# Two-layer encoder with top-2 experts in fp32: slot selections from spread slot numbers, slot weights as row sums, whole weight loads, and two sets of dummy matmuls in the S5 mixer

## What is computed

```python
def _hier_moe(h, w_group, b_group, w_expert, b_expert, w_gate, w_up, w_down):
    ...
    combine = (jax.nn.one_hot(g_idx[:, 0], N_GROUPS, dtype=jnp.float32)[:, :, None]
               * g_val[:, :, None] * within[:, None, :]).astype(h.dtype)
    y = jnp.zeros_like(t)
    for g in range(N_GROUPS):
        a = jnp.einsum('td,edf->tef', t, w_gate[g])
        u = jnp.einsum('td,edf->tef', t, w_up[g])
        act = jax.nn.silu(a) * u * combine[:, g, :, None]
        y = y + jnp.einsum('tef,efd->td', act, w_down[g])
```

## Time and profile before

| | |
|---|---|
| median of 3 runs | 852.99 us (852.57 to 853.74) |
| profiled execution | 855.27 us, its span 853.50 us |
| mean granted TensorE clock | 0.971 |
| TensorE busy | 784.3 us (92%), 4303 matmul records |
| VectorE (DVE) / ScalarE (ACT) / GpSimd (POOL) busy | 379.1 / 282.5 / 143.8 us |
| moved by DMA | 245.54 MB, mean 288 GB/s |

### The profile page before, as it was taken

One profiled execution on the slowest core, in us unless ns is written; L12 is line 12 of the kernel. 1 busy time (PEld: TensorE's weight loads), 2 busy tenths in 40 slices (PEclk: granted clock), 3 DMA queues, 4 the chain that ended last, 5 costly groups with the idle time before them and its releaser, 6 DMA issues.

```text
span 853.5 us, 11150 instructions
## 1 busy us (share of the span) xinstructions
PE 784.3 (92%) x4303; PEld 425.0 (50%) x4303; DVE 379.1 (44%) x701; ACT 282.5 (33%) x522; POOL 143.8 (17%) x135
## 2 busy tenths in 40 slices
PE   3867979999999999989999878998999999999997
PEld 3645845534343343436888644555434434344355
DVE  6998633631222212217868669526222221231164
ACT  5250153521212212216755444433322221221163
POOL 5695510110000000000066554000000000000000
PEclk9896989999999999999999979999999999999999
DMA  6052096799999999997579490266799999999931
GB/s 223 1 156 99 4 327 279 284 337 415 412 413 414 411 415 411 412 405 261 197 166 328 124 269 1 79 266 246 260 403 414 412 414 413 412 415 412 410 138 49
DMA packets 73926, 245.54 MB, mean 288 GB/s; under 512 B 16050, under 2 KB 17136, under 8 KB 65296
## 3 DMA queue, kind: packets, MB, share of 16 engines
q1 hardware_dynamic: 71776, 240.35, 73.2%
q0 software_dynamic: 2096, 4.45, 2.9%
HBM read 243.17 MB, written 1.60 MB: 287 GB/s over the span
## 4 chain that ended last, share of the span: by engine, by line
PE 75%; DVE 8%; DMA 6%; SPq 4%; POOL 4%; ACT 2%; issue 2%; DVEq 0%; ACTq 0%
PE PS L1887 22%; PE PS L1915 12%; PE PS L1662 11%; PE PS L1929 5%; DMA ring<-in_p 5%; PE PS L1821 3%; PE PS L2163 3%; PE PS L1776 2%; PE PS L2138 2%; PE PS L2117 2%; PE PS L1836 2%; PE PS L2049 2%; SPq L466 1%; PE PS L1755 1%; POOL qrs L693 1%
## 5 line engine op out<-in xcount | busy, mean ns | idle before, releaser
L1887 PE MATMUL PS<-ring,xw 128*64 128x512 f32 x1024 | 226.2, 593 | 2.9 <-DVE act L1395 1.5
L1887 PEld LDWEIGHTS PS<-ring,xw 128*64 128x64 f32 x1024 | 73.6, 137 | 146.5 <-issue 143.3
L1915 PE MATMUL PS<-ring,actT 128*64 128x512 f32 x512 | 122.4, 603 | 1.3 <-DVE actT L1389 0.7
L588 POOL TENSOR_TENSOR rstd<-ms,mhalf 128x2 f32<-128x2 f32 x6 | 4.3, 710 | 570.7 <-DVE ms L1053 564.5
L902 ACT ACTIVATE ohi<-PS 128x512 fp32r<-128x512 f32 x64 | 38.2, 597 | 160.4 <-PE PS L1915 160.4
L1389 DVE COPY actT<-PS 128x256 f32<-128x256 f32 x32 | 13.6, 424 | 166.7 <-PE PS L1898 159.1
L1078 DVE SCALAR_TENSOR_TENSOR ringr<-ring,gcol,dwh 128x512 fp32r<-128x512 f32 x80 | 62.7, 834 | 26.9 <-ACT dwh L753 25.8
L1403 DVE TENSOR_TENSOR olo<-PS,ohi 128x512 fp32r<-128x512 f32 x64 | 44.1, 689 | 67.1 <-ACT ohi L902 65.7
L894 ACT ACTIVATE act<-PS,wslot 128x256 f32<-128x256 f32 x32 | 15.2, 474 | 158.9 <-PE PS L1887 158.9
L753 ACT ACTIVATE dwh<-ring,gcol 128x512 fp32r<-128x512 f32 x80 | 52.8, 716 | 35.0 <-PE PS L1662 34.2
L1662 PE MATMUL PS<-ringr,hTh 128*128 128x512 f32 x160 | 63.2, 395 | 0.0
(11 more groups left out here) (332 smaller groups left out, 1067.2 us busy)
## 6 DMA issues: line engine op xcount, KB each, us to landing
ring<-in_moe_w_gate SPq DMA_DIRECT2D x128, 512.0 KB, 15.9
ring<-in_moe_w_up SPq DMA_DIRECT2D x128, 512.0 KB, 16.4
ring<-in_moe_w_down SPq DMA_DIRECT2D x64, 1024.0 KB, 17.0
ring<-in_nat_w_qkv SPq DMA_DIRECT2D x6, 2048.0 KB
ring<-in_ple_w_gate SPq DMA_DIRECT2D x4, 2048.0 KB
ring<-in_s_w_out SPq DMA_DIRECT2D x2, 2048.0 KB
ring<-in_nat_w_o SPq DMA_DIRECT2D x2, 2048.0 KB
ring<-in_s_w_in SPq DMA_DIRECT2D x1, 2048.0 KB
```

What stands on the lines that cost most here:

```text
L1887: ins = mm(PS[CAP * h_:CAP * h_ + CAP, 0, :].rearrange("p (u f) -> p u f", u=2), xw[:, p % 2, k, CAP * h_:CAP * h_ + CAP], wv[h_][:, k], s ...
L1915: ins = mm(PS[CAP * h_:CAP * h_ + CAP, 2 + n, :], actT[:, k, CAP * h_:CAP * h_ + CAP], wd[h_][:, k, 512 * n:512 * n + 512], start=k == 0, ...
```

## The change

Selections: TensorE spreads the slot numbers of all tokens over the partitions once a layer (`slot_rows`: a matmul of the slot column, repeated 128 times, with the identity), DVE keeps them in `slotrow`. For a pair DVE compares them with the number of the slot that a partition stands for (`pid`) and so has the transposed selection without a transpose. Slot weights: token weights and norms are spread in the same way (`weight_rows`), and a slot's weight is the sum of a row, accumulated while selection and row are multiplied. `MIX` and its semaphores go. SP: gate and up are loaded whole, except for pairs 3 and 4. The transposes of p move behind down(15). POOL: an iota and a copy for `pid`, and the router of layer 1 loaded behind the norm of PLE 0, since `rstdrow` now lies where the router does. S5: two sets of `keep_busy(4)`.

```diff
             def load_early(n):
 
                 s, (gate_, up_, _) = items[n]
-                if prev[n] is not None:
-                    name, value = done[prev[n]]
-                    sp.wait_ge(S("gu_half" if name == "gu_done" else name), value)
                 sp.dma_start(ring[s][:, 0:1024], gate_[1][:, 0:1024]).then_inc(loaded[s], 32)
                 sp.dma_start(ring[s][:, 2048:3072], up_[1][:, 0:1024]).then_inc(loaded[s], 16)
...
+            def load_gate_up(n):
                 s, (gate_, up_, _) = items[n]
                 if prev[n] is not None:
                     name, value = done[prev[n]]
                     sp.wait_ge(S(name), value)
+                sp.dma_start(ring[s][:, 0:2048], gate_[1]).then_inc(loaded[s], 32)
+                sp.dma_start(ring[s][:, 2048:4096], up_[1]).then_inc(loaded[s], 16)
...
-                    if p < NP:
+                    if p in (3, 4):
+                        sp.wait_ge(S("gu_half"), 2 * i + p - 2)
                         load_early(m0 + 2 * p)
                         load_early(m0 + 2 * p + 1)
-                        load_late(m0 + 2 * p)
-                        load_late(m0 + 2 * p + 1)
+                        sp.wait_ge(S("gu_done"), NP * i + p - 2)
+                        load_late(m0 + 2 * p, late_loaded[p - 3])
+                        load_late(m0 + 2 * p + 1, late_loaded[p - 3])
+                    elif p < NP:
+                        load_gate_up(m0 + 2 * p)
+                        load_gate_up(m0 + 2 * p + 1)
...
+            link(pool.iota(pid_i[:, :], pattern=[[P, NP]], base=0, channel_multiplier=1))
+            pool.tensor_copy(pid[:, :], pid_i[:, :])
...
+            norm_pow(2)
+            link(pool.memset(wr[:, :, NG:8], 0.0))
             load_router(pool, 1)
             router_gain(1)
-            norm_pow(2)
             norm_pow(3)
...
             def silu(i, p):
                 ac.wait_ge(S("gu_done"), NP * i + p + 1)
-                q, o_ = divmod(p, 2)
-                if p == 0:
-                    ac.wait_ge(S("st0_ready"), 2 * i + 1)
...
+                ac.wait_ge(S("wslot_ready"), NP * i + p + 1)
...
+            def rows(i):
+
+                ve.wait_ge(S("rows_done"), 2 * i + 1)
+                link(ve.tensor_copy(slotrow[:, :, :].rearrange("p j t -> p (j t)"), PS[:, 7, :]))
+                ve.wait_ge(S("rows_done"), 2 * i + 2)
+                ve.tensor_copy(rstdrow[:, :], PS[:, 4, T:2 * T])
+                link(ve.tensor_copy(wrow[:, :, :].rearrange("p j t -> p (j t)"), PS[:, 6, :]))
+
+            def slot_weights(i, p):
+
+                for n, row in enumerate((wrow[:, 0, :], wrow[:, 1, :], rstdrow[:, :], rstdrow[:, :])):
+                    link(stt(act[:, p % 2].rearrange("p k f -> p (k f)"), slotrow[:, n % 2, :], pid[:, p:p + 1], row,
+                             ALU.is_equal, ALU.mult, accum_out=wpart[:, p % 2, n % 2, n // 2:n // 2 + 1]))
+                tt(wslot[:, p % 2, :], wpart[:, p % 2, 0, :], wpart[:, p % 2, 1, :], ALU.add).then_inc(S("wslot_ready"), 1)
+
+            def select(i, p):
+
+                n = NP * i + p
+                if n >= 2:
+                    ve.wait_ge(S("comb_done"), n - 1)
+                link(ts(selT[:, p % 2, :], slotrow[:, 0, :], pid[:, p:p + 1], None, ALU.is_equal))
+                stt(selT[:, p % 2, :], slotrow[:, 1, :], pid[:, p:p + 1], selT[:, p % 2, :].bitcast(F32), ALU.is_equal,
+                    ALU.add).then_inc(S("selT_ready"), 1)
...
                 for p in range(NP):
-                    q, o_ = divmod(p, 2)
                     if p:
                         actT_evict(i, p - 1)
                     gate(i, p)
-                    if q + 1 < NQ:
-                        if o_:
-                            selT_evict(i, q + 1)
-                        else:
-                            weights_evict(i, q + 1)
+                    if p + 1 < NP:
+                        slot_weights(i, p + 1)
                     if p:
                         out_lo(i, p - 1)
-                    if o_ and q + 2 < NQ:
-                        select(i, q + 2)
+                    select(i, p)
...
+            pe.wait_ge(S("WT_ready"), 16)
+            pe.wait_ge(S("consts"), 1)
+            keep_busy(4)
             pe.wait_ge(S("prod_ready"), 8)
             for n in range(SG // 4):
+                if n == 2:
+                    pe.wait_ge(S("T1_raw"), 2)
+                    keep_busy(4)
...
+            def slot_rows(i):
+
+                pe.wait_ge(S("slot_ready"), i + 1)
+                for j in range(2):
                     for t in range(TT):
...
+                        o_ = T * j + P * t
+                        ins = mm(PS[:, 7, o_:o_ + P], bc(slot[:, j, t], 1, P), ident[:, :], start=True, stop=True)
+                ins.then_inc(S("rows_done"), 1)
+
+            def weight_rows(i):
+
+                pe.wait_ge(S("wgt_ready"), i + 1)
+                for j in range(2):
                     for t in range(TT):
...
+                        o_ = T * j + P * t
+                        mm(PS[:, 6, o_:o_ + P], bc(wgt[:, j, t], 1, P), ident[:, :], start=True, stop=True)
+                pe.wait_ge(S("past_ready"), i + 1)
+                mm(PS[0:1, 4, 0:1], past[:, :], ones[:, 0:1], start=True, stop=True)
+                for t in range(TT):
+                    ins = mm(PS[:, 4, T + P * t:T + P * t + P], bc(rstd[:, (1 + 3 * i) % 2, t], 1, P), ident[:, :],
+                             start=True, stop=True)
+                ins.then_inc(S("rows_done"), 1)
...
                 for k in range(k0, k1):
-                    if k == KD // 2:
-                        late_arrived(pe, moe_item[i] + 2 * p)
+                    if k == KD // 2 and p in (3, 4):
+                        pe.wait_ge(late_loaded[p - 3], 64 * (i + 1))
...
+                slot_rows(i)
                 gate_up(i, 0, 0, 4)
-                slot_weights(i, 0)
-                sel_transposes(i, 0)
...
+                weight_rows(i)
                 gate_up(i, 0, 4, KD)
...
                 act_transposes(i, NP - 1)
                 combine(i, NP - 2)
-                p_transposes(i)
                 down(i, NP - 1, 0)
                 down(i, NP - 1, 1)
+                p_transposes(i)
                 combine(i, NP - 1)
```

## The result

The changed kernel took 861.21 us in the median of 11 runs (856.51 to 863.95), the kernel before 854.15 us beside it on the same chip (11 runs, 850.10 to 857.54). The ratio, taken over all the runs, is 1.0079, 95% interval 1.0052 to 1.0105: slower by some 6.7 us (the medians differ by 7.1). Forecast were 846.8 us, 842 to 852.5. The sign was wrong, and the range missed.

What follows compares the result with a forecast made beforehand. The weight queue, not TensorE's pace, was taken to bound the expert stages. S5's -6.0, layer 0's -0.4 and layer 1's +0.2 gave -6.2 us: 849.1 for the profiled execution, 846.8 as median, range 842 to 852.5.

Steps and rivals of the forecast that it cites:

- What bounds the kernel: Expert stages: the weight queue is slower than TensorE and sets the end; TensorE's pace in between doesn't count.
- The rate: Expert stages, pairs 5 to 15: whole loads in 8 KB rows move 426 instead of 410 GB/s, -4.2 us a layer.
- keep_busy in S5, -6.0 us: S5: dummy matmuls keep TensorE's clock full, so the state outputs start at 94.9 and not at 100.81.
- The rival that the clock in S5 doesn't hold: S5: full clock is lost at the zeroing; gain of 0 to 2 us or cost up to 3.5; chance 0.15.
- one of 2.8 (48.9 to 51.7) left it at 1.00: S5: TensorE's clock stayed full after an idle of 2.8 us.
- the rival of the falling clock: Expert stages: the refill starves or the clock falls in new gaps; 849 to 852 us; chance 0.13.
- The cover of the refill: Layer start: 4 us of stream left when pair 4 is issued hide pair 1's delay of about 1.4 us.
- about equal: Layer start: seven matmuls in place of 21 after the first half of pair 0's gate_up take about the same time.
- the lost half: Last pair: TensorE can't begin on half the weights, which eats the gain in rate, leaving -0.2 us.
- End of a layer: Moving p's transposes behind the last down delays the last combine by 2.15 us; totals -0.4 and +0.2 us by layer.
- The credit for p, -2.4 and -1.8: End of layers 0 and 1: moving p's transposes removes TensorE's wait for p and 0.67 us ahead of down.
- Spread at the start, +0.6 a layer: Layer start: four matmuls spreading slot numbers ahead of gate_up of pair 0 delay everything behind, +0.6 us a layer.

Runs made afterwards that it cites:

- run 6: The changed kernel with gate and up loaded in halves again, as in the kernel before: 860.3 us, ratio 1.0079 to the kernel before.
- run 2: The kernel before with only the whole loads of gate and up (pairs 3 and 4 in halves): 847.31 us, ratio 0.9948.
- run 11: The kernel before with whole loads, p's transposes behind the last down and ACT's order turned, old selections kept: 847.05 us, ratio 0.9931.
- run 10: Two kernels: the last kernel of run 9 without the S5 dummies, ratio 0.9983; and the kernel before once more, 853.75 us.
- run 5: The changed kernel with the function table for silu loaded early on ACT: 857.75 us, ratio 1.0063 to the kernel before.
- Run 8: The changed kernel with three dummy matmuls ahead of gate_up of pair 1 and of pairs 12 to 15: 854.96 us, ratio 1.0021.
- the last kernel of run 9: The changed kernel with ACT's order turned, early silu table, pair 5 in halves, three dummies ahead of gate_ups of pairs 12 to 15: ratio 0.9967.

## Why the prediction was wrong

- **What bounds the kernel** was right. Rounds of 12.67 us appeared, ended in waits, and brought nothing.
- **The rate** was right in kind, 421 and not the 426 GB/s that I took. Two kernels that differ in these loads alone show it (run 6: 412, the changed kernel: 421), and in run 2 the last gate_up starts 3.4 and 3.3 us sooner after that of pair 0 than the last half did in before, where the sum had 4.2. By the Trainium skill (DMA: Bandwidth & Descriptors, Specifications), which has line rate from 512 B up, there should have been no difference; the runs say otherwise, and the measurement decides.
- **keep_busy in S5, -6.0 us**, failed, an error of 6.1 us. The step was "An idle of 3.0 us (72 to 75) is followed by half clock", read from one execution and taken for a rule. An idle of 2.97 us at that place was followed by half clock in the trace of before, and one of 2.98 us by full clock in that of run 11, which has the same S5 code:

```profile
75.46 2.06 PE L1783 MATMUL PS<-s5V,s5W 64*128 64x128 f32 x32 [2.98 <-issue]
```

  Alone the dummies measured +0.1 us (-1.5 to +1.6). The rival that the clock in S5 doesn't hold came true in a part of the executions, with the dummies (this is the timeline of after) and without them (79.65 in run 10): one T group of 3.68 us in place of 2.06 behind the zeroing. That the zeroing is the reason isn't shown: in nine of the twelve traces with the dummies this group ran at full clock.

```profile
77.78 2.06 PE L1766 MATMUL PS<-s5V,s5W 64*128 64x128 f32 x32
...
82.25 3.68 PE L1766 MATMUL PS<-s5V,s5W 64*128 64x128 f32 x32
```
- **"one of 2.8 (48.9 to 51.7) left it at 1.00"** is the step that made the rival of the falling clock too small (0.13, "1 to 2.5 a layer come through", all of it at gate_ups). Ahead of gate_ups, waits of 2.36 and 2.37 us were followed by half clock in 8 of 8 cases (four kernels), and those of 1.98 to 2.14 us in 10 of 17 (five kernels); one of 2.22 us (run 5) was not. Run 8 prices it at 5 us in all, the combine's share included, for which I had no term.
- **The cover of the refill** failed. "of pair 3's 4.19 MB only 2.4 go from 173 to 181 at 303 GB/s" was read from before; now that stretch moves 368 GB/s, the stream ran out of work, and the delay of pair 1, costed at nothing, made a hole. Part of the delay was the seven matmuls between the halves of gate_up of pair 0, forecast as "about equal": the second half starts 5.43 us after the first, not 4.70. The first 30 us from gate_up of pair 0 on moved 317 GB/s in before's windows and 274 in after's, 1.29 MB less, or 3.1 us at 421. The hole from 181 to 185 is 0.8 MB of it, and there is a second slack stretch, from 186 to 192, another 0.8 MB below before's, with the DMA engines' share at 0.91 (first line after's 30 us, then 186 to 192 in after and in before):

```profile
166.67:196.67 30.00, 27.02 (x123) 10.40 (x124) 12.17 (x40) 7.75 (x13) 1.33 (x2) 0.94 0.76 274
186.00:192.00 6.00, 5.39 (x26) 1.98 (x24) 3.55 (x12) 1.63 (x3) 0.00 (x0) 1.00 0.91 264
...
186.00:192.00 6.00, 6.00 (x31) 2.08 (x29) 3.02 (x7) 2.47 (x4) 0.00 (x0) 1.00 1.02 403
```

  The second one stays where the first is mended (313 GB/s from 185 to 191 in the last kernel of run 9), and no run here says what makes it. Against run 2, which has the same loads, the last gate_up starts 2.6 and 2.3 us later (197.18 for 194.57 us after gate_up of pair 0, 197.17 for 194.91). Most of what the whole loads had won is gone, with the lost half on top: the last gate_up ends 2.7 and 2.4 us later after that of pair 0 than in before, where the forecast had 0.8 earlier. Over both layers that is an error of 6.7 us, as large as that of S5.
- **End of a layer.** The idle came as forecast (1.99 us; combine begins 2.67 us after the last down). The half clock behind it had no term: combine took 3.15 us (385.65 to 388.80) in place of 1.91, and with proj it cost 1.6 a layer. The credit for p, -2.4 and -1.8, came too: from the end of the last gate_up to the last down it is 8.39 us in both layers, against 10.80 and 10.22. But 1.7 and 1.1 of it the whole loads bring by themselves (run 2), so the move of p was credited with what it didn't earn. Counted from the end of the last gate_up, its new place is worth 0.5 us a layer (run 11 against run 2; their times overlap).
- **Spread at the start, +0.6 a layer**: +0.9. From the last matmul of `gather` to gate_up of pair 0 it is 1.21 us in after and 0.32 in before, in both layers. So one of the theory's rivals, the extra work ahead of gate_up of pair 0, holds for 1.8 us of the loss.
- The sum: forecast -6.2, measured +6.7. S5 is 6.1 of the difference; the stages, where -1.4 was forecast and +6.9 is in the trace, another 8.3; the fall that reaches into proj 1.5, and the spreading 0.6. That is 16.5 for the 12.9 to be explained. Most of the rest is the choice of the execution: three traces of the old stages sum to 436.7, 438.1 and 440.4 us, and against their mean the new ones are +5.2 and not +6.9; and the profiled execution of after was 2.4 us above its median, that of before 1.1.

## What to carry to other kernels

Where a queue sets the end of a stage, cutting TensorE's work buys only waits, and a wait near 2 us may also cost the clock for what follows; keep the work, or take the wait away. After moving an operation on one engine, go through the other engines' orders for who now waits for it: here one line of ACT cost the most. And a clock that fell in one profiled execution is no term of a sum until a second execution shows it.

## What the runs showed of the hardware

- At the same place of the same S5 code and behind the same idle (2.97 and 2.98 us) the clock was half in one execution (before) and full in another (run 11).
- A gate_up of 7.09 us behind a wait took 8.65 to 8.79 where the clock fell: 1.6 to 1.7 us, never the 3.5 that I had put down for half clock throughout. One T group (3.68 for 2.06) and the combine with proj (1.6) lost as much; in S5 of before two groups and the zeroing between them ran at half clock in a row.
- Gate and up in rows of 8 KB in place of 4 KB: 421 for 412 GB/s, with the down rows the same in both. The number of DMAs halves with it.
- An accumulated row sum on DVE is one pass of 0.48 us and an accumulator read of 0.08.
